# Moving the lo parts of the weights from GpSimd to VectorE in a two-layer decoder step

## What is computed

```
x += 0.5 * post(swiglu_1(pre(x)))         # width 2816
z  = pre(x) @ w_in                        # 24 column tiles of 128
A  = dilated window attention(z), 6 heads # prompt; samples read a cache of 2048
B  = conv(4) -> RG-LRU recurrence, times gelu gate
C  = mLSTM matrix memory, 4 heads, in chunks of 128 tokens
x += post(concat(norm A, norm B, norm C) @ w_out)
x += 0.5 * post(swiglu_2(pre(x)))
x += post(sigmoid(pre(x) @ w_ple_gate) * (p @ w_ple_proj))
```

## Time and profile before

| | |
|---|---|
| median of three runs | 2516.7 us (2514.28, 2516.7, 2519.93) |
| the profiled execution | 2516.3 us, span 2514.6 us |
| mean granted clock of TensorE | 0.973 |
| busy: TensorE | 2393.9 us |
| busy: VectorE | 1035.3 us, 1585 instructions |
| busy: ScalarE | 828.8 us |
| busy: GpSimd | 877.2 us, 382 instructions, of which 364 lo parts: 867.9 us |
| read from memory | 238.68 MB, 98 GB/s |

### The profile page before, as it was taken

The page is one execution under the profiler, slowest core; times in us unless marked ns, Lnnn a source line. Parts: engine busy times, 40 slices in busy tenths (PEclk is TensorE's granted clock), DMA queues, the critical chain, the costliest instruction groups (busy, mean ns, idle before and its releaser), DMA issues.

```text
span 2514.6 us, 43095 instructions
## 1 busy us (share of the span) xinstructions
PE 2393.9 (95%) x18938; PEld 2296.6 (91%) x18938; DVE 1035.3 (41%) x1585; ACT 828.8 (33%) x1333; POOL 877.2 (35%) x382
## 2 busy tenths in 40 slices
PE   7999999999898999999899999999998999999996
PEld 7999999988678999999899999989885789999996
DVE  4333304764538333203673331057544473332046
ACT  4222223331445222223442222244214452222243
POOL 3443443431013434343233434424210234343431
PEclk9999999999899999999999999999888999999998
DMA  3222222221651222322222222222117422223221
GB/s 142 93 83 92 91 98 86 84 82 41 244 190 65 95 92 84 101 93 93 74 69 90 84 91 90 95 77 92 66 56 281 155 76 83 91 84 101 93 84 53
DMA packets 74467, 247.44 MB, mean 98 GB/s; under 512 B 14424, under 2 KB 16736, under 8 KB 74336
## 3 DMA queue, kind: packets, MB, share of 16 engines
q1 hardware_dynamic: 74336, 245.59, 28.8%
HBM read 238.68 MB, written 6.88 MB: 98 GB/s over the span
## 4 chain that ended last, share of the span: by engine, by line
PE 80%; DVE 14%; ACT 4%; issue 1%; DMA 0%; POOL 0%; SPq 0%; DVEq 0%; ACTq 0%
PE psum L529 66%; PE psum L546 4%; PE psum L822 2%; DVE x L1475 2%; DVE xl L1467 1%; PE psum L885 1%; DVE acc L1461 1%; DVE y_z L1989 1%; PE psum L919 1%; DVE y_ff L1472 1%; DVE sqx L1490 1%; ACT sq L1079 1%; PE psum L690 1%; PE psum L857 1%; DVE y_z L1472 1%
## 5 line engine op out<-in xcount | busy, mean ns | idle before, releaser
L2014 POOL TENSOR_TENSOR wl<-raw,wh 128x1024 fp32r<-128x1024 f32 (+2 forms) x364 | 867.9, 2386 | 1540.3 <-ACT wh L1072 1540.3
L529 PE MATMUL psum<-xh,wh 128*128 128x272 f32 x3472 | 731.0, 292 | 20.0 <-DVE z L1608 11.8
L1072 ACT CAST wh<-raw 128x1024 fp32r<-128x1024 f32 (+2 forms) x364 | 374.0, 1029 | 1069.6 <-PE psum L529 968.9
L529 PE MATMUL psum<-xh,wl 128*128 128x272 f32 x3472 | 724.2, 290 | 0.0
L529 PE MATMUL psum<-xl,wh 128*128 128x272 f32 x3472 | 721.9, 290 | 0.0
L529 PEld LDWEIGHTS psum<-xh,wh 128*128 128x128 f32 x3472 | 552.9, 190 | 25.5 <-DVE z L1608 13.6
L529 PEld LDWEIGHTS psum<-xl,wh 128*128 128x128 f32 x3472 | 551.9, 191 | 0.0
L529 PEld LDWEIGHTS psum<-xh,wl 128*128 128x128 f32 x3472 | 548.0, 191 | 0.0
L1505 DVE TENSOR_TENSOR hl<-act_out,hh 128x544 fp32r<-128x544 f32 x88 | 218.5, 2483 | 92.7 <-ACT hh L1117 92.7
L529 PE MATMUL psum<-hh,wl 128*128 128x272 f32 x1232 | 255.0, 288 | 0.0
L529 PE MATMUL psum<-hh,wh 128*128 128x272 f32 x1232 | 254.7, 288 | 0.0
(11 more groups left out here) (261 smaller groups left out, 2384.0 us busy)
## 6 DMA issues: line engine op xcount, KB each, us to landing
raw<-in_weights SPq DMA_DIRECT2D x340, 512.0 KB, 3.5
kv<-in_kc SPq DMA_DIRECT2D x32, 672.0 KB, 7.6
kv<-in_vc SPq DMA_DIRECT2D x32, 672.0 KB, 6.7
raw<-in_weights SPq DMA_DIRECT2D x16, 320.0 KB, 4.9
raw<-in_weights SPq DMA_DIRECT2D x8, 384.0 KB, 5.6
x<-in_x SPq DMA_DIRECT2D x4, 544.0 KB, 7.0
out_x<-x SPq DMA_DIRECT2D x8, 272.0 KB, 2.1
out_v<-z SPq DMA_DIRECT2D x2, 816.0 KB, 4.3
```

The source lines that it names most:

```text
L529: ins = pe.matmul(T(t)[:, h, :], w, r[:, h, :], start=first and n == 0, stop=last and n == 2)
L1072: act.copy(wh[:, G % RING, 0:n], raw[:, G % 2, 0:n]).then_inc(hi.sem, 1)
L2014: po.tensor_tensor(wl[:, G % RING, 0:n], raw[:, G % 2, 0:n], wh[:, G % RING, 0:n].bitcast(F32), ALU.subtract).then_inc(lo.sem, 1)
```

## The change

VectorE gets a function `weight_lo`, with the same subtraction, and calls it at some sixty stated places of its program. POOL loses `lo_parts` and keeps the masks and the `memset`. Loads, hi parts, matmuls and buffers stay as they are. The places, in words: two chunks and then one after each half of the first `xl` at the start; in `gate_up` one behind the gate product and one behind `hl`; in `out_tiles` two before an eviction and one behind it; in the joins between feature tiles; behind the squares, before the wait for `r2`, in `x_squares` ahead of the mix and of the embedding gate (calls 1 and 3, not 0 and 2); behind z tiles in the mix; in the memory loop behind a z tile and before `finish(t)`; at stated turns of the attention; in `out_a`; and behind each tile's sum of squares in the embedding gate. A chunk beyond the last layer's is skipped.

The diff, cut to its core:

```diff
+            def weight_lo(*chunks):
+                for G in chunks:
+                    if G < DEPTH * X_ALL:
+                        n = width(G)
+                        ve.wait_ge(hi.sem, G + 1)
+                        ve.tensor_tensor(wl[:, G % RING, 0:n], raw[:, G % 2, 0:n], wh[:, G % RING, 0:n].bitcast(F32),
+                                         ALU.subtract).then_inc(lo.sem, 1)
...
-            def x_squares(L, hq):
+            def x_squares(L, hq, G=None):
...
+                if G is not None:
+                    weight_lo(G + RING)
                 ve.wait_ge(r2_ready.sem, r2_ready.at(L, hq + 1))
...
                     ve.tensor_tensor(act_out[:, b], T(2 * b), r2[:], ALU.mult).then_inc(gate_ready.sem, 1)
+                    weight_lo(L * X_ALL + c + 2 * f + RING)
...
                       .then_inc(hl_ready.sem, 1)
+                    weight_lo(L * X_ALL + c + 2 * f + 1 + RING)

             def out_tiles(L, m, y, c):
                 for d in range(KT - 1):
+                    weight_lo(c + 3 * d + RING, c + 3 * d + 1 + RING)
...
                         add_square(L, m, d)
+                    weight_lo(c + 3 * d + 2 + RING)
...
-                join(L, 1, Y_OUT, g, 0, range(1, KT), *to_f2)
+                join(L, 1, Y_OUT, g, 0, [1], *to_f2)
+                weight_lo(L * X_ALL + X_F2 + 2)
+                join(L, 1, Y_OUT, g, 0, range(2, KT), *to_f2)
+                weight_lo(L * X_ALL + X_F2 + 3)
                 join(L, 1, Y_OUT, g, 1, range(KT), *to_f2)
...
+                E = L * X_ALL + X_IN + RING
                 for t in range(3):
                     z_tile(L, t)
+                weight_lo(E + 1)
...
                 z_tile(L, 12)
+                weight_lo(E + 12)
...
                     z_tile(L, E_MEM + t)
+                    weight_lo(E + E_MEM + t)
                     finish(t)
...
+            weight_lo(0, 1)
             for h in range(2):
                 for k in range(KT):
...
+                weight_lo(2 + h)
...
-                join(L, 0, Y_FF, g, 0, range(4), *to_mix)
+                c = G + X_D1 + 3 * (KT - 1) + RING
+                join(L, 0, Y_FF, g, 0, [0], *to_mix)
+                weight_lo(c)
+                join(L, 0, Y_FF, g, 0, [1], *to_mix)
+                weight_lo(c + 1)
+                join(L, 0, Y_FF, g, 0, [2, 3], *to_mix)
                 last_half(L, 0, Y_FF, G + X_D1, 1)
                 join(L, 0, Y_FF, g, 0, range(4, KT), *to_mix)
+                weight_lo(c + 2)
                 join(L, 0, Y_FF, g, 1, range(KT), *to_mix)
-                x_squares(L, 1)
+                x_squares(L, 1, G + X_IN)
...
-                x_squares(L, 3)
+                x_squares(L, 3, G + X_PG)
...
                     if d:
                         add_square(L, 3, d)
+                    if 0 < d < KT - 2:
+                        weight_lo(G + X_PG + d + RING)
...
-                lo_parts(L * X_ALL, L * X_ALL + X_IN + E_MEM + 4)
...
-                lo_parts(L * X_ALL + X_OB + 3, (L + 1) * X_ALL)
```

More of the change, by code:

```diff
@@ L1539, in out_a @@
                         add_square(L, 1, d)
+                    if d == 2:
+                        weight_lo(L * X_ALL + X_F2)
                 to_f2 = (L, N_F2, G_F2PRE)
@@ L1635, in mix_vector @@
                     if tap in (3, 1):
-                        z_tile(L, 3 if tap == 3 else 4)
+                        e = 3 if tap == 3 else 4
+                        z_tile(L, e)
+                        weight_lo(*((E + 2, E + 3) if e == 3 else (E + 4,)))
                 ins.then_inc(xc_ready.sem, 1)
                 z_tile(L, 5)
+                weight_lo(E + 5)
                 ve.tensor_copy(sb_[:, S_CP:S_CS].rearrange("p (j t) -> p j t", j=3), z[:, 0:3, SEQ - 3:SEQ])
@@ L1649, in mix_vector @@
                     z_tile(L, e)
+                    weight_lo(E + e)
                 ve.wait_ge(rg_ready.sem, rg_ready.at(L, 6))
@@ L1652, in mix_vector @@
                 z_tile(L, 10)
+                weight_lo(E + 10)
                 ve.wait_ge(ab_ready.sem, ab_ready.at(L, 2))
@@ L1657, in mix_vector @@
                 z_tile(L, 11)
+                weight_lo(E + 11)
                 ve.wait_ge(bs_ready.sem, bs_ready.at(L, 1))
@@ L1675, in mix_vector @@
                 z_tile(L, 13)
+                weight_lo(E + 13)
                 ve.wait_ge(b_done.sem, b_done.at(L, 1))
@@ L1714, in mix_vector @@
                 ve.tensor_tensor(dw_s, m0b, gg_s, ALU.subtract).then_inc(row_ready.sem, 1)
+                weight_lo(E + 14)
                 z_tile(L, E_TURN)
@@ L1720, in mix_vector @@
                 ve.tensor_copy(gc[0:32, 4, :], psum[0:32, 6, 16:20]).then_inc(gc_ready.sem, 1)
+                weight_lo(E + E_TURN)
                 z_tile(L, E_ROWS)
+                weight_lo(E + E_ROWS)
                 z_tile(L, E_ROWS + 1)
+                weight_lo(E + E_ROWS + 1)
                 ve.wait_ge(wb_ready.sem, wb_ready.at(L, 4))
@@ L1804, in mix_vector @@
                 weigh_sample(1)
+                weight_lo(E + E_MEM + 4)
                 z_tile(L, E_MEM + 5)
@@ L1878, in mix_vector @@
                             early_lo(L, 3 + c)
+                        weight_lo(L * X_ALL + X_OB + 3)
                     if 2 <= i < PAIRS + 2:
@@ L1883, in mix_vector @@
                           .then_inc(o_ready.sem, 1)
+                    if i >= 5 and i % 2:
+                        weight_lo(L * X_ALL + X_OB + 4 + (i - 5) // 2)
                     for g in range(2):
@@ L1934, in mix_vector @@
                 evac(FILL_END)
+                weight_lo(L * X_ALL + X_OA + 1)
                 ve.wait_ge(gr_ready.sem, gr_ready.at(L, 4))
@@ L1979, in _ @@
                 g, to_ple = dc2[:, L, D_HALF2:D_HALF2 + 8], (L, N_PLE, G_PLEPRE)
-                join(L, 2, Y_FF, g, 0, range(4), *to_ple)
-                last_half(L, 2, Y_FF, G + X_D2, 1)
-                join(L, 2, Y_FF, g, 0, range(4, KT), *to_ple)
+                c = G + X_D2 + 3 * (KT - 1) + RING
+                join(L, 2, Y_FF, g, 0, [0], *to_ple)
+                weight_lo(c)
+                join(L, 2, Y_FF, g, 0, [1], *to_ple)
+                weight_lo(c + 1)
+                join(L, 2, Y_FF, g, 0, [2, 3], *to_ple)
+                last_half(L, 2, Y_FF, G + X_D2, 1)
+                join(L, 2, Y_FF, g, 0, [4], *to_ple)
+                weight_lo(c + 2)
+                join(L, 2, Y_FF, g, 0, [5, 6], *to_ple)
+                weight_lo(c + 3)
+                join(L, 2, Y_FF, g, 0, [7], *to_ple)
+                weight_lo(c + 4)
                 join(L, 2, Y_FF, g, 1, range(KT), *to_ple)
-                x_squares(L, 3)
+                x_squares(L, 3, G + X_PG)
                 for d in range(KT - 1):
@@ L2001, in _ @@
                 to_f1 = (L + 1, N_F1, G_F1PRE) if L + 1 < DEPTH else ()
-                for h in range(2):
-                    join(L, 3, Y_Z, pc2[:, L, G_PLEPOST:G_PLEPOST + 8], h, range(KT), *to_f1)
+                g = pc2[:, L, G_PLEPOST:G_PLEPOST + 8]
+                join(L, 3, Y_Z, g, 0, range(5), *to_f1)
+                weight_lo(G + X_PG + KT - 1 + RING)
+                join(L, 3, Y_Z, g, 0, range(5, KT), *to_f1)
+                join(L, 3, Y_Z, g, 1, range(KT), *to_f1)
                 steps.end()
@@ L2008, in _ @@
         def _(po):
[L2009 to L2015, removed]
             for L in range(DEPTH):
                 steps = Steps(po, pool_steps, L)
-                lo_parts(L * X_ALL, L * X_ALL + X_IN + E_MEM + 4)
                 for t in range(5):
-                    if t >= 2:
-                        G = L * X_ALL + X_IN + E_MEM + t + 2
-                        lo_parts(G, G + 1)
                     n = P if t < 4 else 32
```

5 lines of the change are left out of this document (4 added, 1 removed).

## The result

The changed kernel takes 2495.0 us (median of six runs, 2492.3 to 2498.2) against 2516.7 before: 21.7 us less, a ratio of 0.9914 (95% interval 0.9901 to 0.9926). The profiled execution took 2492.3 us, its span is 2490.6.

The account below looks back on a forecast made before the run. The prediction took TensorE, busy 95% of the span, as the bound, so only its 120.7 us of idle time could shrink. Terms summed to -8.8 us, from 2516.3 to 2507.5 us, range 2497 to 2520.

Parts of the forecast that it names:

- startup: At the start, TensorE's longest wait for a lo part, 5.1 us for the third chunk, gets shorter: -1.5 us.
- fifth tiles: In each of four feed-forward pieces, TensorE's fifth tile starts 1.2 us later, nothing covering it: +4.8 us.
- joins and convolution: From down to mix, lo parts and hi-part waits replace held VectorE instructions: -1.4 and -1.3, twice each, -5.4 us.
- recurrence: In the mix, TensorE's 3.0 us wait for an evicted z tile goes: -3.0 us a layer, -6.0 in all.
- memory loop: A lo part waiting for ACT's cast delays finish(2) by 3.9 us; TensorE pays 1.1 with attention's share: +2.2 in two layers.
- output projection: Up to the second feed-forward, five lo parts replace 9.1 us of held instructions: -0.9 us a layer, -1.8 in all.
- embedding gate, with the join before it: At each layer's end, shorter waits outweigh longer tile chains: -1.1 us in layer 0, about 0 in the last.
- Start of each feed-forward part: The fifth chunk's lo part now stands behind the first gate product, so the fifth tile starts 1.22 us later.
- Feed-forward parts worth nothing: Inside the four unbroken TensorE pieces of 356.56 us, faster VectorE work is hidden: 0 us.
- the clock: TensorE's granted clock: a gap of 2 to 3 us may cost 0, 1.7 or 3.4 us more than itself.
- Rival 1: More gain: removed recurrence and embedding gaps take slow stretches along, memory stall stays hidden: 2498.5 us, half 2502; chance 0.20.
- Rival 3, slower by new gaps: Eight new gaps at feed-forward starts, joins to the mix and last embedding tiles drop the clock: 2521 to 2535 us; chance 0.13.

Follow-up runs that it names:

- e7: Changed kernel with the embedding gate's lo parts moved behind the next tile's product, into VectorE's wait for the sigmoid: 2486.7 us.
- e4: Changed kernel, but POOL again makes the lo parts inside the four feed-forward parts: 2491.8 us.
- e1: The kernel before, unchanged, run for a second profile: single time 2519.5 us.
- e3: Changed kernel with lo parts recomputed on VectorE to bring back three earlier gaps (recurrence, output projection, embedding; the last did not come): 2511.4 us.
- e5: Changed kernel with only the recurrence's gap given back, one lo part computed four times on VectorE: 2507.5 us.
- e6: Changed kernel with only the output projection's gap given back, one lo part computed twice and ahead of the last eviction: 2499.8 us.
- e9: Kernel of e7 with the lo part for the embedding gate's sixth chunk computed twice, to make a gap: 2489.3 us.
- e11: Changed kernel, but POOL makes the lo parts of the memory loop and the attention: 2498.2 us.
- e12: Kernel before, but VectorE makes the lo parts of the memory loop and the attention only: 2519.0 us, against 2516.4 in its runs.
- e8: Changed kernel with three places of lo parts moved: embedding gate, each feed-forward part's fifth chunk, the memory loop's third one: 2479.5 us.

## Why the prediction was wrong

Most steps of the sum held. By comparing TensorE's waits in the two profiles, one by one at the same matmul:

| step | predicted us | measured us |
|---|---|---|
| startup | -1.5 | -0.6 |
| fifth tiles | +4.8 | +4.2 |
| joins and convolution | -5.4 | -5.9 |
| recurrence | -6.0 | -6.1 |
| memory loop | +2.2 | +2.1 |
| output projection | -1.8 | -2.3 |
| embedding gate, with the join before it | -1.1 | -0.9 |
| behind the last matmul, and pieces under 0.1 us | 0 | +0.3 |
| sum | -8.8 | -9.2 |

- *Startup*: wrong. The wait that was to get shorter, 5.1 us for the third chunk, stayed at 5.2; a second one, of 1.2, went, and the first matmul came 0.4 later.
- *Start of each feed-forward part*: right, on the line. Answering to the earlier trace rows, the product, the lo part behind it, and TensorE:

```profile
1275.78 0.72 DVE L1511 TENSOR_TENSOR act_out<-psum,r 128x544 f32<-128x544 f32 x1 [4.29 <-ACT r L1092]
1276.42 1.22 DVE L1457 TENSOR_TENSOR wl<-raw,wh 128x1024 fp32r<-128x1024 f32 x1
...
1277.69 0.52 PE L529 MATMUL psum<-xh,wh 128*128 128x272 f32 x2 [1.80 <-DVE wl L1457]
```

- *Memory loop*: right. Answering to the earlier trace rows, VectorE waits 5.94 us for a cast ahead of `finish(2)`, and TensorE pays 0.95 of it:

```profile
595.57 0.83 DVE L1457 TENSOR_TENSOR wl<-raw,wh 128x640 fp32r<-128x640 f32 x1 [5.94 <-ACT wh L1072]
596.31 0.42 DVE L1797 SCALAR_TENSOR_TENSOR dn<-psum,em 128x256 f32<-128x256 f32 x1
...
601.25 0.32 PE L702 MATMUL psum<-z 64*32 64x32 f32 x8 [0.95 <-DVE at L1771]
```

- *Embedding gate*: the net agrees by luck. The terms written for layer 0 (-1.9, -1.2, 5 x 0.5, -1.6, and 2.1 less 1.2) add up to -3.1, not to the -1.1 that went into the sum; with -3.1 the forecast would have been 2505.5. Measured were -0.9 in layer 0 and 0.0 in layer 1, from larger parts: tiles were 5.0 us apart, and by the last one TensorE waited 5.77 us for the sum of squares in layer 0; e7 took that away.

```profile
1236.42 0.82 PE L552 MATMUL psum<-acc,con 128*128 128x272 f32 x1 [5.77 <-DVE acc L1470]
```

- *Feed-forward parts worth nothing*: right, shown by e4.
- **The step that failed is the clock.** "A gap of 2 to 3 us may cost 0, 1.7 or 3.4 us more than itself" stood in the text, and the forecast then put in 0. It measured 12.5 us in the medians, 14.8 in the profiles. Rival 1 priced this at 6.8 us, for the gaps of the recurrence and the embedding, and came to 2498.5; the range ended just below that. It left out the output projection, where the wait in the summing of squares fell from 3.36 us to 1.34 in both layers, and it took layer 0's recurrence for safe because one profile had shown no slow stretch there; e1 showed one. Nothing in the prediction priced the clock in the memory loop and the attention, where 6.9 of the 14.8 us stand. What is shown: the gaps of the recurrence and the output projection, given back without POOL, bring slow stretches with them (e3, e5, e6), 7.2 us beyond the waits in e3. e9's clock rows make the embedding a cause too, but its time is within the error. What made the memory loop and the attention faster stays open (e11 and e12). The wait in layer 0's output projection, before and after:

```profile
770.94 0.82 PE L552 MATMUL psum<-acc,con 128*128 128x272 f32 x1 [3.36 <-DVE acc L1461]
...
758.22 0.50 PE L552 MATMUL psum<-acc,con 128*128 128x272 f32 x1 [1.34 <-DVE acc L1470]
```

- *Rival 3, slower by new gaps*: the four at the fifth tiles came, 1.8 us each; they do bring slow stretches, but cheap ones (2.3 us on average, see e8). The two of 3.3 us in the joins to the mix did not come: the longest wait there went from 2.5 to 2.3. At the last embedding tiles came 5.77 us in layer 0 and 2.90 in layer 1. The 5.77 us stand in a stretch with a granted clock of 0.55, that is 0.45 x 2 x 19 = 17 us at 1.2 GHz, half of it with TensorE at work (9.5 us busy in 19):

```profile
1231.00:1250.00 19.00, 9.50 (x29) 6.94 (x30) 12.09 (x24) 10.80 (x22) 0.00 (x0) 0.55 0.19 56
```

## What to carry to other kernels

Where one engine is 95% busy, sum the waits of that engine place by place, and give each gap of about 2 us or more that comes or goes a second price, the slow clock behind it: for the gaps of the recurrence and the output projection it was 7.2 us beside 9.2 of waiting (e3). That price is an average over executions, so take it from several profiles. Where an operation is held by a neighbour's instruction, ask which of the held ones stand on the path; 260 of 364 moves gained nothing, and the 104 between the large pieces gained all. In an engine that works in order, put a helper's work into a wait that it has anyway, not behind the step that others wait for: three such moves gave a further 15.5 us.

## What was not expected of the hardware

A gap that one profile shows without a slow stretch has one in the next: the same kernel's recurrence in layer 0 read 1.00 and 0.87. TensorE's busy time stayed within 1.5 us all the same, so two profiles of each kernel are worth their price when gaps of 2 to 4 us are in question. Shorter gaps do it as well: behind 1.8 us a piece of 356.6 us took 358.1 in 14 of 36 cases, and behind 0.75 us in none of 20. The runs of one kernel spread by 0.6 us (e4, four runs) to 11.8 (e5: 2503.7 to 2515.5, seven runs), while the waits of two profiles differ by 1.2 and 1.7.
